# Chunked RWKV-7 scan on TensorE: operands laid out by each head's partition half, and products issued over four 64x64 tiles of the array

## The chip, the cores and the metric

The kernel runs on one core of a Trainium2 chip. A core has a matrix engine (TensorE, PE in the rows), whose weight loads are shown apart as PEld, two engines for elementwise work that can read the matrix engine's result memory PSUM (VectorE or DVE, and ScalarE or ACT), one that works only on SBUF here (GpSimd, POOL), and DMA queues. The metric is the time of one execution in microseconds (us) on the device; lower is better.

## The reference

Two layers of a hybrid backbone over 256 latent and 256 context tokens, width 1024: an input projection feeds three mixers (a bidirectional RWKV-7 scan, attention, a Fourier mix), then a gated merge, an output projection and a feed-forward part. Only the scan is touched by the change. It has 8 heads of width 64, runs in both directions, first over the context, then over the latent tokens from the state reached:

```
def step(S, inp):
    r_t, w_t, k_t, v_t, kk_t, b_t = inp
    sa = -jnp.einsum("bhvk,bhk->bhv", S, kk_t)
    S = S * w_t[:, :, None, :] + sa[..., None] * b_t[:, :, None, :] + v_t[..., None] * k_t[:, :, None, :]
    return S, jnp.einsum("bhvk,bhk->bhv", S, r_t)
S, ys = lax.scan(step, state0, xs, reverse=reverse)
```

The latent stream is returned. The context's outputs y are needed in layer 0 only; in layer 1 the context steps carry the state alone.

## The kernel before, in words

The function scan (from L998) is run once for each of the two layers. It takes the tokens in chunks of 64, so there are 8 steps in a scan (4 context, 4 latent), 16 in all, and each step handles one chunk of each of the two directions d = 0 and 1. A head takes 64 of the 128 partitions, and two heads are a pair: the even head of a pair is on partitions 0 to 63 (UP), the odd one on 64 to 127 (DOWN), and 4 pairs lie side by side. PSUM has 8 banks; direction d owns banks 4d+0 to 4d+3, called B_L, B_LT, B_G, B_S.

One step, for both directions in turn, is on TensorE:

1. **Gram products** (helper `each`, L1259): per pair and head, 64x64 tiles that stay in their partition half (rows UP to outputs UP, DOWN to DOWN). B_LT takes a 128-column product per head, B_L a 64-column one, B_G a 128-column one. Each f32 product is two matmul instructions in the trace, so 8 heads x 2 = 16 instructions for each of the three.
2. **Transposes** (L1296) that turn the decayed keys (BK) token-major into B_S, full 128x128; those of the values (L1305) come later.
3. **The inverse of a unit triangular 64x64 matrix per head**, by merging blocks: T2 holds the inverse and its transpose. The first level is made by DVE (L1198, L1200). Then for levels 1 to 4: X1 = LM x T2 (16 instructions per direction, L1259), ScalarE copies X1 to SBUF (L1120), then two merge products T2 x X1 and X1 x T2 (32 instructions per direction, L1259), and DVE subtracts both from T2 (L1212). The level's mask LM is made by GpSimd (L1064). Level 5 works on 32x32 halves (L1272) and ends in L1217.
4. **The tail**: W = [Q | Gram] x [State ; V] with both parts stacked over all 128 partitions (L1333), ScalarE copies it (L1137); the same stack gives y (L1339); sa = T x W (L1259), copied negated by ScalarE (L1141, two instructions per direction, one for each partition half); y += sa x ARB (L1351); the state product (L1360), stacked over 128 rows and always to outputs UP.
5. DVE adds y (L1236), multiplies the state product by the decay (L1240) and adds the decayed old state (L1243), which GpSimd made at the head of the step (L1056, L1057). These and the stacks need the heads side by side on 64 partitions: tiles QRG, STATE_V, SA_V, BK_TOK, ARB, SD, of which many are written by two instructions, one for each half (`by_head`): L1177 (keep), L1187 (gram_out), L1204, L1141.

All engines follow a program written out by hand in this order; each engine is in order, and semaphores carry the dependences. Within the level loop DVE also does, for direction d, gram_out and keep after levels 1 and 2, the next step's operands(0) (L1168 to L1170) and exponents (L1156, L1157) after the subtraction of level 3, and operands(1) after level 5. ScalarE does its exps (L1088 to L1094) and copies (L1105, L1129, L1134) between the levels. `hold` is a semaphore increment that an engine makes after its waits.

Of the kernel before, what the change touches and what calls it, by code (L numbers as in the profile page):

```python
# [23 lines left out]
ALU = mybir.AluOpType  # L24
AX = mybir.AxisListType

P = 128
# [152 lines left out]
def build_in(ctx, nc, ins, out):  # L180
# [30 lines left out]
    DEC = [sb(f"decay_{d}", [HD, HEADS]) for d in range(NDIR)]  # L211
    DEC_KEPT = [sb(f"decay_kept_{d}", [HD, HEADS]) for d in range(NDIR)]
# [694 lines left out]
    def scratch(*shape):  # L907
# [3 lines left out]
        for i, (mem, at, end) in enumerate(free):  # L911
            if at + n <= end:
# [9 lines left out]
    VF = [scratch(PAIRS, 2, HD) for _ in range(NDIR)]  # L922
    T2 = [scratch(2, PAIRS, HD) for _ in range(NDIR)]
    QRG = [scratch(HEADS, 2, HD) for _ in range(NDIR)]
    STATE_V = [scratch(HEADS, HD) for _ in range(NDIR)]
    SA_V = [scratch(HEADS, HD) for _ in range(NDIR)]
    BK_TOK = [scratch(HEADS, HD) for _ in range(NDIR)]
    ARB = [scratch(HEADS, HD) for _ in range(NDIR)]
    SD = [scratch(HEADS, HD) for _ in range(NDIR)]
# [30 lines left out]
    s_sa_v = [sig(f"values_doubled_{d}") for d in range(NDIR)]  # L960
# [3 lines left out]
    s_add = [sig(f"state_product_decayed_{d}") for d in range(NDIR)]  # L964
    s_ds = [sig(f"state_product_{d}") for d in range(NDIR)]
    s_y_out = [sig(f"y_added_{d}") for d in range(NDIR)]
    s_sd = [sig(f"state_decayed_{d}") for d in range(NDIR)]
# [6 lines left out]
    scan_signals = [s_expo, s_exp, s_init, *s_qr, *s_ops, *s_qr2, *s_gram, *s_lts, *s_gram_out, *s_bk_tok, *s_bk_turned, *s_v_turned, *s_add, *s_v, *s_v_tok, *s_sa_v, *s_lm, *s_x1, *s_x1_out,  # L974
                    *s_tx, *s_t, *s_w, *s_w_out, *s_sa, *s_sa_out, *s_y, *s_ds, *s_y_out, *s_sd, *s_st, *s_first, *s_arb]
# [22 lines left out]
    def scan(context_y):  # L998
# [30 lines left out]
        def of_head(h, half):  # L1029
# [3 lines left out]
        B_L, B_LT, B_G, B_S = 0, 1, 2, 3  # L1033
        by_head = lambda tile, h: (tile.rearrange("p (j h) t -> p j h t", h=2)[:, :, h] if len(tile.shape) == 3 else
                                   tile.rearrange("p (j h) q t -> p j h q t", h=2)[:, :, h])
        pairs = lambda bank, a: BANK[:, bank, a:a + HALF].rearrange("p (j t) -> p j t", j=PAIRS)
        with stage() as block:
            @block.gpsimd
            def _(pool):
                def operands(i, t, d):  # L1040


                    pool.wait_ge(*at_step(s_gram[d], i, 3))
# [5 lines left out]
                def step(i, need_y, more):  # L1049
                    t = [tokens(pool, d, i + 1) for d in range(NDIR)] if more else None  # L1050
                    for d in range(NDIR):

                        pool.wait_ge(*at_step(s_st[d], i))
                        pool.wait_ge(*at_step(s_exp, i, 2, d + 1))
                        hold(pool, "pool")
                        nc.gpsimd.tensor_copy(DEC_KEPT[d][:], DEC[d][:])  # L1056
                        s_sd[d].mark(nc.gpsimd.tensor_tensor(SD[d][UP], STATE_V[d][UP], DEC[d][:].unsqueeze(2).to_broadcast([HD, HEADS, HD]), ALU.mult))  # L1057
# [1241 lines left out]
```

## Time and profile before

| quantity | value |
|---|---|
| median of 3 runs | 2362.63 us (2360.34 to 2364.29) |
| the profiled execution | 2364.6 us, of which the span is 2362.8 us |
| granted TensorE clock over the span, mean | 0.943 |
| busy: PE / PEld / DVE / ACT / POOL | 88% / 70% / 49% / 35% / 14% |
| windows that hold the 16 scan steps, both layers | 513.1 us |

A row of a timeline gives the start, the duration of the merged group, engine, line, operation, tiles written and read, the shape and the count; the bracket is the idle time of the engine just before it and what ended it. A group of pipelined instructions lasts from the first one's start to the last one's end.

### The profile page before, as it was taken

What the parts mean: (1) busy time and instruction counts of PE and PEld (TensorE: products, weight loads), DVE (VectorE), ACT (ScalarE), POOL (GpSimd) and SP (SyncE); (2) the same over time, 40 slices, a digit from 0 to 9 for tenths busy, and PEclk for the clock granted to TensorE, in tenths of its full rate; (3) what the DMA queues carried; (4) which work ended last, traced back from release to release, by engine and by line L of the source; (5) the groups of instructions that cost most, each with busy time, mean ns of one, the idle gap of its engine ahead of it and who ended that gap; (6) DMA issues with size and microseconds to landing.
All of it is one profiled execution on the core that took longest, in us unless ns stands there. A gap on an engine that the chain in (4) does not pass through costs nothing. (4 is left out here: it accounts for less than half of the span.)

```text
span 2362.8 us, 46800 instructions
## 1 busy us (share of the span) xinstructions
PE 2087.1 (88%) x19559; PEld 1657.3 (70%) x19559; DVE 1169.0 (49%) x1849; ACT 832.9 (35%) x1515; POOL 340.5 (14%) x444
## 2 busy tenths in 40 slices
PE   4886888879989999889998998968888798988998
PEld 2653888843557887668886665748887456988988
DVE  1644778762562333253332216377877435545544
ACT  1343444423442222242221114354443244434432
POOL 1112333301100011010001001043332020010000
PEclk8997999989989999999999998979999899999999
DMA  7425000030111332223226743000001211553553
GB/s 263 152 85 200 1 0 2 1 127 13 36 51 49 92 106 89 72 71 107 90 89 238 282 154 125 27 2 0 1 1 44 96 36 56 170 179 125 185 172 126
DMA packets 144521, 219.40 MB, mean 93 GB/s; under 512 B 6846, under 2 KB 123800, under 8 KB 137216
## 3 DMA queue, kind: packets, MB, share of 16 engines
q1 hardware_dynamic: 142880, 215.74, 26.9%
q8 instruction: 101, 1.65, 0.3%
q0 software_dynamic: 1504, 1.71, 0.2%
q14 instruction: 36, 0.29, 0.0%
HBM read 208.00 MB, written 9.44 MB: 92 GB/s over the span
## 5 line engine op out<-in xcount | busy, mean ns | idle before, releaser
L367 PE MATMUL BANK<-H_high,W_high 128*128 128x512 f32 (+2 forms) x1472 | 524.2, 356 | 70.6 <-ACT H_high L630 32.3
L331 DVE TENSOR_TENSOR W_low<-RING,W_high 128x1024 fp32r<-128x1024 f32 x268 | 328.2, 1234 | 461.9 <-ACT W_high L328 461.9
L368 PE MATMUL BANK<-H_low,W_high 128*128 128x512 f32 (+2 forms) x1472 | 520.0, 353 | 0.0
L369 PE MATMUL BANK<-H_high,W_low 128*128 128x512 f32 (+2 forms) x1472 | 519.0, 353 | 0.0
L328 ACT ACTIVATE W_high<-RING 128x1024 fp32r<-128x1024 f32 x268 | 279.3, 1052 | 613.8 <-PE BANK L369 585.9
L367 PEld LDWEIGHTS BANK<-H_high,W_high 128*128 128x128 f32 (+1 forms) x1472 | 283.8, 193 | 117.0 <-issue 50.5
L368 PEld LDWEIGHTS BANK<-H_low,W_high 128*128 128x128 f32 (+1 forms) x1472 | 284.0, 193 | 38.0 <-issue 1.1
L369 PEld LDWEIGHTS BANK<-H_high,W_low 128*128 128x128 f32 (+1 forms) x1472 | 283.7, 193 | 38.0
L1259 PE MATMUL BANK<-RING,WORK 64*64 64x64 f32 x4096 | 166.4, 220 | 16.7 <-DVE RING L1212 8.8
L1259 PEld LDWEIGHTS BANK<-RING,WORK 64*64 64x64 f32 x4096 | 145.2, 134 | 29.2 <-issue 29.0
L1064 POOL TENSOR_TENSOR WORK<-WORK,masks 128x256 f32<-128x256 f32 x160 | 125.5, 796 | 116.5 <-PE BANK L1259 114.7
L367 PE MATMUL BANK<-hidden_high,W_high 128*128 128x512 f32 (+1 forms) x352 | 122.4, 348 | 12.0 <-PEq L2066 12.0
L368 PE MATMUL BANK<-hidden_low,W_high 128*128 128x512 f32 (+1 forms) x352 | 120.0, 341 | 0.0
L369 PE MATMUL BANK<-hidden_high,W_low 128*128 128x512 f32 (+1 forms) x352 | 120.0, 341 | 0.0
L1259 PE MATMUL BANK<-WORK,RING 64*64 64x64 f32 x2560 | 108.1, 225 | 3.1 <-issue 0.7
L2004 POOL TENSOR_TENSOR merge_tiles<-merge_tiles 128x512 f32<-128x512 f32 (+1 forms) x32 | 33.9, 1068 | 480.7 <-DVE merge_tiles L1986 480.7
L1120 ACT ACTIVATE WORK<-BANK 128x256 f32<-128x256 f32 (+1 forms) x160 | 56.5, 362 | 131.5 <-PE BANK L1259 123.5
L1259 PEld LDWEIGHTS BANK<-WORK,RING 64*64 64x64 f32 x2560 | 93.9, 139 | 8.3 <-issue 6.8
L1212 DVE TENSOR_TENSOR RING<-RING,BANK 128x512 f32<-128x512 f32 x128 | 83.7, 683 | 31.9 <-PE BANK L1259 29.1
L1259 PE MATMUL BANK<-RING 64*64 64x128 f32 (+1 forms) x1536 | 79.5, 263 | 21.1 <-DVE RING L1170 21.1
L367 PEld LDWEIGHTS BANK<-hidden_high,W_high 128*128 128x128 f32 x352 | 67.9, 193 | 34.9 <-issue 27.7
L1259 PEld LDWEIGHTS BANK<-RING 64*64 64x64 f32 x1536 | 75.6, 141 | 22.9 <-issue 21.9
(281 smaller groups left out, 3113.9 us busy)
## 6 DMA issues: line engine op xcount, KB each, us to landing
modulation_weights<-w_mod_dram SPq DMA_DIRECT2D x48, 1024.0 KB, 6.7
RING<-w_in_dram SPq DMA_DIRECT2D x46, 1024.0 KB, 5.9
RING<-w_ffn_in_dram SPq DMA_DIRECT2D x44, 1024.0 KB, 5.1
RING<-w_ffn_out_dram SPq DMA_DIRECT2D x20, 1024.0 KB, 5.1
RING<-w_out_dram SPq DMA_DIRECT2D x8, 1024.0 KB, 5.3
h_high<-H_high SPq DMA_DIRECT2D x2, 2048.0 KB, 7.5
h_low<-H_low SPq DMA_DIRECT2D x2, 2048.0 KB, 13.2
H_high<-h_high SPq DMA_DIRECT2D x2, 2048.0 KB, 11.8
```

What stands on the lines that cost most here:

```text
L328: high_ready.mark(nc.scalar.activation(self.part(0, c), self.raw(c), ACT.Copy))
L331: low_ready.mark(nc.vector.tensor_tensor(self.part(1, c), self.raw(c), self.part(0, c).bitcast(FP32), ALU.subtract))
L367: nc.tensor.matmul(out, w[0], x[0], start=start, stop=False)
L368: nc.tensor.matmul(out, w[0], x[1], start=False, stop=False)
L369: return nc.tensor.matmul(out, w[1], x[0], start=False, stop=stop)
L1064: s_lm[d].mark(nc.gpsimd.tensor_tensor(LM[d], LTS[d], lanes(level_mask(d, l)), ALU.mult))
L1120: s_x1_out[d].mark(nc.scalar.activation(X1[d][:, :, cols], pairs(4 * d + B_L, 0)[:, :, cols], ACT.Copy))
L1212: s_t[d].mark(nc.vector.tensor_tensor(T2[d].rearrange("p q j t -> p (q j t)"), T2[d].rearrange("p q j t -> p (q j t)"), BANK[:, 4 * d + B_ ...
L1259: last = nc.tensor.matmul(BANK[rows, bank, at + j * stride:at + j * stride + width], lhs(j)[rows], rhs(j)[rows], start=True, stop=True)
L2004: pool_sig.mark(nc.gpsimd.tensor_tensor(total(m), total(m), gate(u), ALU.add))
```

## The change

The stacks over 128 partitions are given up. Each tile of the scan keeps the even heads of the pairs on one partition half and the odd ones on the other, so most copies and elementwise instructions that were two of 64 partitions become one of 128 partitions with half the elements per partition. What was one product over K = 128 becomes two accumulated products over K = 64, one of each head's own half and one whose operands have the heads of a pair exchanged (GRAM_X, V_X, the second half of BK_TOK, and the transposed inverse T2[:, 1]). The helper side_by_side interleaves up to two products, pair by pair. A product is given by the pair (rows, outputs): STAY reads and writes the same half, CROSS goes from the own half to the other, BACK from the other to the own, STAY_OTHER is STAY with the halves named the other way round. A STAY and a CROSS (or BACK) product together use all four 64x64 tiles of the array, in two banks.

The transposes become products with an identity (eye_heads). The state decay is one multiplication by DVE after one addition, and GpSimd's two instructions per direction (L1056, L1057) are gone. New waits of TensorE on its own products: s_turned_1, s_turned_2, s_w_1, s_y_1, s_y_2, s_ds_1, and two on the first gram product.

```diff
-                for h, rows in enumerate((UP, DOWN)):
-                    last = nc.vector.tensor_copy(by_head(QRG[d][UP], h), QR[d][rows])
-                s_qr2[d].mark(last)
+                s_qr2[d].mark(nc.vector.tensor_copy(QR_KEPT[d], QR[d]))
...
-                s_sd[d].mark(nc.gpsimd.tensor_tensor(SD[d][UP], STATE_V[d][UP], DEC[d][:].unsqueeze(2).to_broadcast([HD, HEADS, HD]), ALU.mult))
...
+                        if l >= 4:
+                            d = l - 4
+                            act.wait_ge(*at_step(s_st[d], i))
+                            s_dec[d].mark(nc.scalar.activation(DEC[d][:].unsqueeze(2), INCL[d][:, :, bass.ds(here[d] + (CHUNK - 1), 1)], ACT.Exp, scale=-KAPPA))
...
-                        s_add[d].mark(nc.vector.tensor_tensor(STATE_V[d][UP], BANK[UP, 4 * d + B_S].rearrange("p (g t) -> p g t", g=HEADS),
-                                                              DEC_KEPT[d][:].unsqueeze(2).to_broadcast([HD, HEADS, HD]), ALU.mult))
+                        s_add[d].mark(nc.vector.tensor_tensor(STATE[d], STATE[d], pairs(4 * d + B_S, 0), ALU.add))
...
-                        s_st[d].mark(nc.vector.tensor_tensor(STATE_V[d][UP], STATE_V[d][UP], SD[d][UP], ALU.add))
+                        s_st[d].mark(nc.vector.tensor_tensor(STATE[d], STATE[d], DEC[d][:].unsqueeze(2).to_broadcast([P, PAIRS, HD]), ALU.mult))
...
+                OWN, OTHER = (UP, DOWN), (DOWN, UP)
+                STAY, CROSS, BACK, STAY_OTHER = (OWN, OWN), (OWN, OTHER), (OTHER, OWN), (OTHER, OTHER)
+                def side_by_side(width, *products):
+                    last = [None] * len(products)
+                    for j in range(PAIRS):
+                        for x, (bank, at, (rows, to), lhs, rhs, start, stop) in enumerate(products):
+                            for h in range(2):
+                                last[x] = nc.tensor.matmul(BANK[to[h], bank, at + j * width:at + (j + 1) * width], lhs(j)[rows[h]], rhs(j)[rows[h]],
+                                                           start=start and (j == 0 or stop), stop=stop and (j == PAIRS - 1 or start))
+                    return last
...
+                    first_free(0)
+                    s_gram[0].mark(side_by_side(HD, lower(0))[0])
+                    wide(0)
+                    first_free(1)
+                    pe.wait_ge(*at_step(s_gram[0], i, 4, 1))
+                    across, straight = side_by_side(HD, upper_across(0), lower(1))
+                    wide(1)
+                    pe.wait_ge(*at_step(s_gram[1], i, 4, 1))
+                    across, straight = side_by_side(HD, upper_across(1), (B_S, 0, STAY, bk(0, 0), eye, True, True))
+                    pe.wait_ge(*at_step(s_turned_1, i, 1, 1))
+                    across, straight = side_by_side(HD, (B_S, HALF, CROSS, bk(0, 1), eye, True, True), (4 + B_S, 0, STAY, bk(1, 0), eye, True, True))
+                    pe.wait_ge(*at_step(s_turned_2, i, 1, 1))
+                    s_bk_turned[1].mark(side_by_side(HD, (4 + B_S, HALF, CROSS, bk(1, 1), eye, True, True))[0])
...
+                        if l >= 4:
+                            s_ds_1[d].mark(side_by_side(HD, (4 * d + B_S, 0, BACK, lambda j: BK_TOK[d][:, 1, j], lambda j: V_X[d][:, j], True, False))[0])
...
-                                each(4 * d + B_LT, 0, HD, lambda j: T2[d][:, 1, j], lambda j: X1[d][:, j])
-                                s_tx[d].mark(each(4 * d + B_LT, HALF, HD, lambda j: X1[d][:, j], lambda j: T2[d][:, 1, j]))
+                                s_tx[d].mark(side_by_side(HD, (4 * d + B_L, 0, STAY_OTHER, lambda j: X1[d][:, j], lambda j: T2[d][:, 1, j], True, True),
+                                                          (4 * d + B_LT, 0, BACK, lambda j: T2[d][:, 1, j], lambda j: X1[d][:, j], True, True))[1])
...
+                    s_w_1.mark(side_by_side(HD, w_own(0, True), w_other(1, True))[1])
+                    if need_y:
+                        s_y_1.mark(side_by_side(HD, y_own(0, True), y_other(1, True))[1])
+                    pe.wait_ge(*at_step(s_w_1, i, 1, 1))
+                    one, zero = side_by_side(HD, w_own(1, False), w_other(0, False))
+                    if need_y:
+                        s_y_2.mark(side_by_side(HD, y_own(1, False), y_other(0, False))[1])
...
-                            last = nc.tensor.matmul(BANK[UP, 4 * d + B_S, g * HD:(g + 1) * HD], BK_TOK[d][:, g], SA_V[d][:, g],
-                                                    start=True, stop=True)
+                        s_ds[d].mark(side_by_side(HD, (4 * d + B_S, 0, STAY, lambda j: BK_TOK[d][:, 0, j], lambda j: SA[d][:, j], False, True))[0])
```

wide(d) is the side-by-side form of the two 128-column gram products (B_LT by STAY, B_G by CROSS), 32 instructions. B_LT and B_L have changed numbers (0 and 1), and T2's first level is now read from B_L alone, where the transposed part lies in the second half of the bank with the heads exchanged.

## Rows read from the trace of the kernel before

**Rows 1.** The page: busy time by engine, over the whole span.
```profile
PE 2087.1 (88%) x19559; PEld 1657.3 (70%) x19559; DVE 1169.0 (49%) x1849; ACT 832.9 (35%) x1515; POOL 340.5 (14%) x444
```

**Rows 2.** Windows, one scan step each: us, busy by engine, granted clock, DMA.
```profile
323.50:356.00 32.50, 29.12 (x723) 26.87 (x721) 24.39 (x43) 13.73 (x36) 11.71 (x16) 0.95 0.00 0
418.90:450.10 31.20, 27.68 (x724) 25.47 (x720) 24.45 (x43) 13.73 (x36) 11.71 (x16) 1.00 0.00 0
1664.00:1693.50 29.50, 25.89 (x667) 23.81 (x664) 24.02 (x42) 13.73 (x36) 11.72 (x16) 1.00 0.00 0
```

**Rows 3.** Timeline of one step, its head: gram products, first level, transposes.
```profile
418.37 4.40 PEld L1259 LDWEIGHTS BANK<-RING 64*64 64x64 f32 x96
...
422.95 0.85 PEld L1296 LDWEIGHTS BANK<-ident,RING 128*128 128x128 f32 x8 [0.17 <-issue]
423.64 0.60 ACT L1105 ACTIVATE WORK<-BANK 128x512 f32<-128x512 f32 x1 [1.01 <-PE BANK L1296]
424.35 0.42 PEld L1305 LDWEIGHTS BANK<-ident,RING 128*128 128x128 f32 x4 [0.55 <-issue]
424.94 0.54 PEld L1259 LDWEIGHTS BANK<-RING,WORK 64*64 64x64 f32 x16 [0.17 <-issue]
```

**Rows 4.** Timeline, levels 1 to 3 of the same step.
```profile
425.67 0.38 ACT L1120 ACTIVATE WORK<-BANK 128x256 f32<-128x256 f32 x1 [1.43 <-PE BANK L1259]
426.47 0.58 PEld L1259 LDWEIGHTS BANK<-WORK,RING 64*64 64x64 f32 x16
426.94 0.58 PEld L1259 LDWEIGHTS BANK<-RING,WORK 64*64 64x64 f32 x16
427.79 0.69 DVE L1212 TENSOR_TENSOR RING<-RING,BANK 128x512 f32<-128x512 f32 x1 [1.13 <-PE BANK L1259]
428.68 0.57 PEld L1259 LDWEIGHTS BANK<-RING,WORK 64*64 64x64 f32 x16 [0.23 <-issue]
429.34 1.39 DVE L1187 TENSOR_TENSOR RING<-BANK,masks 64x512 f32<-64x512 f32 x2
430.77 0.90 DVE L1177 COPY RING<-RING 64x512 f32<-64x512 f32 x2
431.70 1.28 DVE L1212 TENSOR_TENSOR RING<-RING,BANK 128x512 f32<-128x512 f32 x2
432.60 1.08 PEld L1259 LDWEIGHTS BANK<-RING,WORK 64*64 64x64 f32 x32 [0.20 <-issue]
```

**Rows 5.** Timeline, level 4 of the same step and the start of level 5.
```profile
436.45 1.08 PEld L1259 LDWEIGHTS BANK<-RING,WORK 64*64 64x64 f32 x32 [0.63 <-issue]
436.75 0.42 DVE L1168 TENSOR_TENSOR RING<-WORK 128x256 f32<-128x256 f32 x1
439.16 0.41 DVE L1157 TENSOR_TENSOR WORK<-WORK 128x256 f32 x1
440.38 0.86 PEld L1272 LDWEIGHTS BANK<-RING,WORK 32*32 32x32 f32 x32 [0.71 <-issue]
441.98 0.53 PEld L1272 LDWEIGHTS BANK<-RING,WORK 32*32 32x32 f32 x32 [0.74 <-issue]
```

**Rows 6.** Timeline, the tail of the same step.
```profile
442.55 1.01 PEld L1333 LDWEIGHTS BANK<-WORK,RING 128*64 128x64 f32 x32
444.56 1.01 PEld L1259 LDWEIGHTS BANK<-WORK,RING 64*64 64x64 f32 x32
445.29 1.56 ACT L1141 ACTIVATE WORK<-BANK 64x256 f32<-64x256 f32 x4 [1.16 <-PE BANK L1259]
447.61 1.94 PEld L1360 LDWEIGHTS BANK<-WORK 128*64 128x64 f32 x32
```

**Rows 7.** Windows of 1 us around level 5 of an earlier step.
```profile
344.00:345.00 1.00, 0.44 (x15) 0.30 (x11) 1.00 (x3) 0.77 (x3) 0.00 (x0) 1.00 0.00 0
346.00:347.00 1.00, 0.36 (x27) 0.39 (x29) 0.00 (x0) 0.95 (x4) 0.63 (x1) 1.00 0.00 0
349.00:350.00 1.00, 1.00 (x24) 1.00 (x20) 0.53 (x2) 0.00 (x0) 0.00 (x0) 0.50 0.00 0
```

More of the change, by code:

```diff
@@ L210, in build_in @@
     g2_sb = sb("g2_sb", [P, WIDTH])
-    DEC = [sb(f"decay_{d}", [HD, HEADS]) for d in range(NDIR)]
-    DEC_KEPT = [sb(f"decay_kept_{d}", [HD, HEADS]) for d in range(NDIR)]
+    DEC = [sb(f"decay_{d}", [P, PAIRS]) for d in range(NDIR)]
     BANK = ctx.enter_context(nc.psum_tensor("BANK", [P, 8, 512], FP32))
@@ L921, in build_in @@
     BK = [scratch(PAIRS, 2, HD) for _ in range(NDIR)]
-    VF = [scratch(PAIRS, 2, HD) for _ in range(NDIR)]
+    VF = [scratch(PAIRS, HD) for _ in range(NDIR)]
     T2 = [scratch(2, PAIRS, HD) for _ in range(NDIR)]
[L924 to L929, printed above, removed]
+    QR_KEPT = [scratch(PAIRS, 2, HD) for _ in range(NDIR)]
+    GRAM_X = [scratch(PAIRS, 2, HD) for _ in range(NDIR)]
+    STATE = [scratch(PAIRS, HD) for _ in range(NDIR)]
+    V_X = [scratch(PAIRS, HD) for _ in range(NDIR)]
+    SA = [scratch(PAIRS, HD) for _ in range(NDIR)]
+    BK_TOK = [scratch(2, PAIRS, HD) for _ in range(NDIR)]
+    ARB = [scratch(PAIRS, HD) for _ in range(NDIR)]
     EXPO = scratch(2, PAIRS, HD)
@@ L1139, in step @@
                         act.wait_ge(*at_step(s_sa[d], i, 1, 1))
-                        for h, rows in enumerate((UP, DOWN)):
-                            last = nc.scalar.activation(by_head(SA_V[d][UP], h), pairs(4 * d + B_LT, 0)[rows], ACT.Copy, scale=-1.0)
-                        s_sa_out[d].mark(last)
+                        s_sa_out[d].mark(nc.scalar.activation(SA[d], pairs(4 * d + B_LT, 0), ACT.Copy, scale=-1.0))
                 for d in range(NDIR):
@@ L1271, in halves @@
                             k = of_head(h, k_rows)
-                            last = nc.tensor.matmul(BANK[of_head(h, out_rows), bank, at + j * HD + out_cols.start:at + j * HD + out_cols.stop],
+                            last = nc.tensor.matmul(BANK[of_head(h ^ across, out_rows), bank, at + j * HD + out_cols.start:at + j * HD + out_cols.stop],
                                                     lhs[k, j, out_rows], rhs[k, j, out_cols], start=True, stop=True)
@@ L1303, in step @@
                             hold(pe)
-                            for j in range(PAIRS):
-                                last = nc.tensor.transpose(BANK[:, 4 * d + B_S, j * P:(j + 1) * P], VF[d][:, j].rearrange("p q t -> p (q t)"), ident[:])
-                            s_v_turned[d].mark(last)
+                            turned = side_by_side(HD, (4 * d + B_S, 0, CROSS, lambda j: VF[d][:, j], eye, True, True))
+                            s_v_turned[d].mark(turned[0])
+                        if l >= 4:
+                            d = l - 4
+                            pe.wait_ge(*at_step(s_v_tok[d], i, 1, 1))
+                            hold(pe)
+                            s_ds_1[d].mark(side_by_side(HD, (4 * d + B_S, 0, BACK, lambda j: BK_TOK[d][:, 1, j], lambda j: V_X[d][:, j], True, False))[0])
                         for d in range(NDIR):
```

153 lines of the change are left out of this document (69 added, 84 removed).

## The prediction

> **What bounds the kernel now.** I read the page first, then windows, then the timeline of one step. TensorE is busy 2087 of 2363 us [rows 1], but in the scan this hides short waits: the windows give 31.2 us for a step at full clock, 32.5 us for one in which the clock was down to 0.95 in the mean, and 29.5 us for a context step of layer 1, which makes no y [rows 2]. DMA moves nothing there. The 16 steps take 513.1 us, 22% of the run, and nothing outside them changes.
>
> The timeline shows a chain, no single busy engine. From the first gram load to the first load of X1 it is 424.94 - 418.37 = 6.57 us [rows 3]. Levels 1 to 4 take 3.74, 3.92, 3.85 and 3.93 us (starts at 424.94, 428.68, 432.60, 436.45, 440.38) [rows 3 to 5], level 5 takes 442.55 - 440.38 = 2.17, and the tail to the next gram product, which follows the state product's end at 447.61 + 1.94, takes 7.05 [rows 5, 6]. Together 31.2 us, the window's length.
>
> **Durations used.** From these rows: a group of 16 matmuls of 64 columns goes out in 426.94 - 426.47 = 0.47 us, 29 ns each [rows 4]. From its first load to ScalarE's copy 425.67 - 424.94 = 0.73 passes, so 0.26 beyond the issue; a copy lasts 0.38 [rows 3, 4]. I add 0.11 from a copy to TensorE (an estimate: about half of DVE's step, below). The two merge groups take 0.94, and DVE starts 1.32 after their first load, so 0.38 beyond the issue; one subtraction is 0.69, two are 1.28, and from its end (428.48) to TensorE's load 0.20 passes [rows 4].
>
> **The unknown: how fast four tiles take matmuls.** Before, groups use two tiles at a time. Three rows bound it. On one column half over all 128 rows (L1360) 32 matmuls take 1.94 us, 61 ns; alternating column halves (L1333) 32 take 1.01, 32 ns with the last one's latency in it; 32-wide ones alternating between two tiles take 0.53 for 32, 16.6 ns [rows 5, 6]. So a second tile halves the interval, two column halves stream different operands over the same rows, and loads and matmuls can leave at 16.6 ns or faster. What no row shows is two row halves that write the same PSUM partitions in different banks at once. Ends: 16.6 ns (issue is then the limit; streaming alone would be 61/4 = 15) and 29 ns (only two tiles ever work). I take 16.6, since L1333 and the L1259 groups each show one of the two directions of the tiling running side by side. A group of 32 then takes 0.53 instead of 0.94, and the 128-column pair, where 96 matmuls took 4.40 [rows 3], so (2.20 - 0.47)/32 = 54 ns each, takes 27 ns x 32 = 0.87 instead of 1.73.
>
> The Trainium skill (TensorE: Matmul & The Clock Gate, section "Wait — 56ns, not 53.3ns?") says that start-to-start never drops below about 25 ns however small the matmul. The L1272 row has 16.6 ns, so the trace does not agree; by the page's floor a merge group would take 0.80, and that is a rival below.
>
> **The change part by part,** a warm latent step:
>
> *Head.* TensorE issues lower(0) 0.47, wide(0) 0.87, upper(0) with lower(1) 0.53, wide(1) 0.87, upper(1) with the first turn 0.53, then a wait on its own product, the second turn 0.53. The self-waits have no row; bounds are 0 and the 0.64 of result latency plus wake-up seen through another engine (0.38 + 0.26); I take 0.35. Sum 4.15. Then ScalarE's copy of BK (0.26 + 0.60 + 0.11 [rows 3]) and the value product 0.47: X1 starts at 5.6 instead of 6.57. T2 is not late: DVE's state update is 4 instructions of 128x256 (0.42 each, as L1168 [rows 5]) instead of 4 of 64x512, and done before wide(1) ends; the first level for d = 0 waits for upper(0) at 1.87 + 0.38, plus two 128x512 instructions of 0.69 = 3.6. GpSimd's mask for level 1 no longer stands behind the state decay. Gain 1.0.
>
> *Levels 1 to 3.* Chain of d = 0: 0.73 + 0.38 + 0.11 + 0.53 + 0.38 + 0.69 + 0.20 = 3.0 us instead of 3.84 in the mean. Of this 0.4 comes from four tiles; the rest was DVE, which reached L1212 late behind gram_out (1.39) and keep (0.90) [rows 4]. These become one instruction each (0.69 + about 0.5), and 1.28 + 1.19 = 2.5 is under the 3.0 of the chain. The second value product sits in TensorE's idle time. Sum 9.0 instead of 11.5; gain 2.5.
>
> *Level 4.* DVE makes operands and exponents before the subtraction: 436.75 to 439.57, 2.82 us [rows 5], unchanged. 1.28 + 2.82 = 4.1: DVE now bounds this level, instead of 3.93. Gain -0.2. The first part of the state product (2 x 0.47) is hidden in TensorE's waiting here; if uncovered it costs 0.9.
>
> *Level 5.* The second product starts 441.98 - 440.38 = 1.60 after the first; the chain alone (0.26 + 0.26 + 0.38 + 0.11) is 1.0. The rest is ScalarE copying SA_V (L1134), which the change removes. Its replacement, one 128x4 exponential per direction, is short. 2.17 - 0.6 = 1.6; gain 0.6.
>
> *Tail.* W takes two groups of 32 with a y group between: W is ready at 3 x 0.53 + 0.26 = 1.85, later than before (0.47 + 0.26). Copy and wake-up 2.35, sa 0.47 + 0.26, its copy is one instruction (0.38) instead of two per direction (1.56 for four [rows 6]), y from 3.57 on 0.94, the state product 2 x 0.47 instead of 1.94. End 5.45 instead of 7.05; gain 1.6. The self-waits on y_1 and w_1 find their product done, except w_1 in a context step without y (0.35).
>
> Sum: 5.6 + 9.0 + 4.1 + 1.6 + 5.45 = 25.8 instead of 31.2, so 5.4 us a step. A step without y saves 4.7 (the y groups it never had, one exposed wait). 12 x 5.4 + 4 x 4.7 = 84 us.
>
> **The clock.** A step whose granted clock fell cost 1.3 us more [rows 2]. It fell to 0.50, which is 1.2 of 2.4 GHz, for some 3 to 4 us after a stretch in which TensorE was busy 0.44 and 0.36 of a microsecond [rows 7]. 8 of the 16 windows show it. The change thins out TensorE's time in the levels (0.94 + 1.06 us of issue in 3.0, instead of 2.8 in 3.85). I count it in all 16 steps: 8 x 1.35 = 11 us back. The profiled execution's 2364.6 less 84 plus 11 is 2292; the median of the runs is 2 us below that execution, and the rate of four tiles is more likely a little under 16.6 ns than over. Forecast 2288 us, 3.2% faster.
>
> **Rivals.**
>
> 1. *Four tiles give nothing* (the change does not do what it says): 29 ns. Head: 0.47 + 1.73 + 0.94 + 1.73 + 0.94 + 0.35 + 0.94, then 1.44 to X1, is 8.5. Levels 1 to 3: 3.44 each, 10.3; level 4 4.1; level 5 1.6; tail 4 x 0.94 + 0.73 + 0.38 + 0.11 + 1.88 = 6.9. Sum 31.4: all that DVE and ScalarE gain is eaten by 208 more matmuls (by the diff, 928 instructions a step instead of 720: the turns 96 instead of 16, W, y and the state product twice as many, the gram 128 instead of 96). 0.2 us a step more with y, about nothing without: 2362 to 2375, with the clock's loss. Against: the rows of L1333. Chance 0.08, half of it within 0.2%, half above.
>
> 2. *An issue floor of 25 ns.* Head 0.47 + 0.87 + 0.80 + 0.87 + 0.80 + 0.35 + 0.80 + 1.44 = 6.4; levels 3.3 each; tail 6.2; sum 28.2, 3.0 us a step, about 2330 with the clock. The Trainium skill's floor (same page) is this case. Against: L1272. For: its burst is short, and nothing shows such a rate held. Chance 0.07.
>
> 3. *Slower: the clock.* If TensorE's thinner work left it at 1.2 GHz for most of each step, everything TensorE issues on the chain doubles: about 4.2 + 0.5 in the head, 1.0 in each of four levels, 3.9 in the tail, 12 to 13 us. The step would be 38, the run 2364.6 + 16 x 6.5 = 2470. It decides from the point where 5.4 of these 12.5 us are lost, so when the low clock holds for over 40% of the scan. Against: in the warm window level 5 has the same thin stretches and 1.00 [rows 2, 5], and each fall seen was over in 4 us [rows 7]. Chance 0.04.
>
> 4. *Better than the sum:* 13 to 15 ns per matmul, no fall of the clock added, and exponents not slowed by GpSimd's work beside them (2.82 us for five 0.42 instructions): another 1 to 1.5 us a step, 2265. That is inside the forecast's own case.
>
> **How the numbers follow.** Forecast with its spread 0.78, floor 0.07, clock 0.04, no gain 0.08, and 0.03 for a stall of TensorE or DVE that I do not see, half of it slower. The range reaches from 2255 (rival 4 with 10 us more) to 2335 (rival 2), and leaves out rivals 1 and 3 and the tails of the forecast. Faster by over 0.2% (4.7 us, about what a measurement of this kernel can tell from none): 0.78 + 0.07 + 0.015 = 0.86; within 0.05; slower 0.09.
>
> **What would show it.** In the changed trace a merge group (32 matmuls of 64x64, BANK<-WORK,RING and RING,WORK mixed) lasts about 0.55 us of loads; 1.0 would be rival 1, 0.8 rival 2. Starts of X1 in consecutive levels 3.0 us apart, 4.1 in level 4 with DVE busy throughout; the tail 5.5. Idle PE of about 0.35 after the first and second turned groups. Wrong would be made by a copy of BK on ScalarE that waits longer than the turns, by a first level on DVE later than 5.4, or by windows with a clock under 0.9.

## The result, and the profile of the changed kernel

The changed kernel takes 2486.43 us (median of 4 runs, 2485.28 to 2488.03) beside 2361.78 us for the kernel before, measured with it: a ratio of 1.053 (95%: 1.051 to 1.055), 5.3% slower. The forecast was 2288 us, its range 2255 to 2335, and "faster" had a chance of 0.86. It was wrong in sign, and by 198 us.

The page of the changed kernel: busy time by engine [rows 1], the line of the granted clock in 40 slices, and the queue that brings instructions.

```profile
PE 2090.4 (84%) x22759; PEld 1659.7 (67%) x22759; DVE 1066.6 (43%) x1753; ACT 774.6 (31%) x1419; POOL 296.8 (12%) x380
...
PEclk8997778988998999999999999867878899998999
...
q8 instruction: 201, 3.29, 0.6%
```

The page of the kernel before, the same two last lines (the first stands in rows 1):

```profile
PEclk8997999989989999999999998979999899999999
...
q8 instruction: 101, 1.65, 0.3%
```

DVE, ScalarE and GpSimd lost the busy time that the change meant to take from them (DVE 1169.0 to 1066.6). TensorE has the same busy sum, 2090 beside 2087, with 3200 more matmuls, which fits four tiles at work. Still the span grew by 121 us, and the instruction queue moved twice as much: 201 packets, 3.29 MB, 16 KB each.

Windows of the two scans and of three single steps (columns as in rows 2: us, busy of PE, PEld, DVE, ACT, POOL, granted clock, DMA share, GB/s). The first two lines are the scans; then, from gram load to gram load, a context and a latent step of layer 0, both with y, and a context step of layer 1, without.

```profile
224.40:538.40 314.00, 226.13 (x7424) 208.67 (x7425) 141.37 (x286) 79.78 (x237) 72.93 (x97) 0.84 0.02 4
1625.20:1939.30 314.10, 226.20 (x7047) 208.60 (x7048) 141.21 (x283) 79.53 (x236) 73.77 (x97) 0.79 0.02 4
...
328.73:373.97 45.24, 29.99 (x928) 27.83 (x928) 16.72 (x36) 10.08 (x30) 8.59 (x13) 0.77 0.02 4
373.97:409.56 35.59, 26.84 (x921) 24.85 (x919) 16.82 (x36) 10.08 (x30) 8.75 (x12) 0.86 0.01 3
1641.52:1680.69 39.17, 26.83 (x839) 24.66 (x836) 17.93 (x34) 10.09 (x30) 9.40 (x13) 0.74 0.02 4
```

The scans take 628.1 us instead of 515.1 (259.1 and 256.0 by the same windows of before), so nearly all of the 121 us is there. The steps shown are 36 to 45 us, where 25.8 had been worked out and 31.2 measured [rows 2]. No engine is busy for more than 30 us of a step.

The waits of TensorE, over the whole span (engine, line, what was waited for: us in all, times, longest):

```profile
PE BANK L1248 <- issue: 129.4, 81, 4.7
...
PE BANK L1257 <- issue: 8.9, 8, 1.5
```

"Issue" is idle time for which no semaphore answers: 138 us, in pieces of up to 4.7 us; all such waits on the scan's lines come to 1.3 us in the kernel before. One piece in detail, in windows of 1 us, two finer windows over the idle time itself, and the timeline (start, us, engine and line, what, and in brackets the wait before it):

```profile
377.00:378.00 1.00, 1.00 (x55) 0.88 (x46) 0.76 (x2) 0.00 (x0) 0.32 (x1) 1.00 0.06 16
...
381.00:382.00 1.00, 1.00 (x32) 1.00 (x33) 0.00 (x0) 0.50 (x2) 0.80 (x2) 0.50 0.00 0
383.00:384.00 1.00, 1.00 (x36) 1.00 (x31) 0.92 (x2) 0.28 (x2) 0.50 (x1) 0.50 0.09 16
...
377.80:378.20 0.40, 0.22 (x8) 0.08 (x4) 0.40 (x2) 0.00 (x0) 0.00 (x0) 1.00 0.14 41
378.20:380.20 2.00, 0.00 (x0) 0.00 (x0) 2.00 (x6) 0.00 (x0) 0.00 (x0) 1.00 0.00 0
```

```profile
377.24 1.28 DVE L1188 TENSOR_TENSOR RING<-RING,BANK 128x512 f32<-128x512 f32 x2 [1.51 <-PE BANK L1248]
380.21 1.53 PEld L1248 LDWEIGHTS BANK<-RING,WORK 64*64 64x64 f32 x34 [2.33 <-issue]
381.03 0.38 ACT L1105 ACTIVATE WORK<-BANK 128x256 f32<-128x256 f32 x1 [4.04 <-PE BANK L1248]
384.27 0.27 PEld L1257 LDWEIGHTS BANK<-RING,WORK 32*32 32x32 f32 x12
386.19 0.45 PEld L1257 LDWEIGHTS BANK<-RING,WORK 32*32 32x32 f32 x20 [1.66 <-issue]
```

TensorE stops for 2.33 us between the first state product and the X1 products of level 4. The only thing that it waits for there is DVE's subtraction, and both of these are done by 378.52; ScalarE, whose 4.04 us also hold its usual wait, stands idle with it. The next stop, 1.66 us, lies in the middle of a group of level 5: 12 loads, the gap, then 20 more with the same operands and no wait between them. A packet of 16 KB starts as the first stop begins (the windows count its bytes where it starts; its own record ends at 378.76), and TensorE goes on 1.4 us after its end. That is no chance: each of the 31 gaps of over 0.9 us between weight loads in this scan (228 to 538 us) ends 1.2 to 1.6 us after the end of a packet of the instruction queue, while these packets come some 5 us apart. After the stop the granted clock falls from 1.00 to 0.50, so the same matmuls take twice as long: 55 matmuls began in the microsecond before the gap, 32 and 36 behind it. That named the suspect, the transport of TensorE's own instructions, and the experiments test it.

### The profile page after: what moved, and what is told of

Read it like the earlier page. It is cut to its first block and busy times, and to the rows that moved or that the text cites. A ratio compares the mean times of both kernels' runs of the same rounds, so it can differ in the third digit from the quotient of the medians.

```text
span 2483.5 us, 52924 instructions
## 1 busy us (share of the span) xinstructions
PE 2090.4 (84%) x22759; PEld 1659.7 (67%) x22759; DVE 1066.6 (43%) x1753; ACT 774.6 (31%) x1419; POOL 296.8 (12%) x380
## 3 DMA queue, kind: packets, MB, share of 16 engines
q8 instruction: 201, 3.29, 0.6%
## 5 line engine op out<-in xcount | busy, mean ns | idle before, releaser
L1248 PE MATMUL BANK<-RING,WORK 64*64 64x64 f32 x4480 | 193.1, 239 | 35.4 <-issue 22.9
L1248 PE MATMUL BANK<-RING 64*64 64x64 f32 (+1 forms) x2944 | 134.6, 308 | 88.4 <-issue 65.1
L1248 PEld LDWEIGHTS BANK<-RING,WORK 64*64 64x64 f32 x4480 | 172.4, 150 | 48.2 <-issue 46.7
L1248 PEld LDWEIGHTS BANK<-RING 64*64 64x64 f32 x2944 | 124.8, 189 | 92.9 <-issue 92.6
L1248 PE MATMUL BANK<-WORK,RING 64*64 64x64 f32 x3072 | 157.8, 257 | 26.7 <-issue 23.1
L1056 POOL TENSOR_TENSOR WORK<-WORK,masks 128x256 f32<-128x256 f32 x160 | 119.4, 759 | 426.3 <-ACT WORK L1097 273.7
L1248 PEld LDWEIGHTS BANK<-WORK,RING 64*64 64x64 f32 x3072 | 134.1, 166 | 35.1 <-issue 34.9
## 6 DMA issues: line engine op xcount, KB each, us to landing
h_low<-H_low SPq DMA_DIRECT2D x2, 2048.0 KB, 12.5
```

Source lines behind the costliest of these rows:

```text
L1056: s_lm[d].mark(nc.gpsimd.tensor_tensor(LM[d], LTS[d], lanes(level_mask(d, l)), ALU.mult))
L1248: last[x] = nc.tensor.matmul(BANK[to[h], bank, at + j * width:at + (j + 1) * width], lhs(j)[rows[h]], rhs(j)[rows[h]], start=start and (j ...
```

## The experiments

**Theory.** The step loop's body, 720 matmuls of code before, is 928 now. It no longer stays on the core, so it is fetched again in every step, and TensorE runs dry. **Rivals:** the clock (rival 3 of the forecast: TensorE's thinner work, not its code); the four tiles themselves (the exchanged halves or two row halves at once); other work of the change.

**The same instructions executed, less code.** Levels 2 to 4 have the same text for TensorE, so they can be an inner loop. 928 matmuls are executed and 736 stand in the code. The order changes a little too: the second value turn moves ahead of the loop, the first part of the state product behind it.

```
+ values_turned(0); level(1, True, False); values_turned(1)
+ Signal.trips = trips * (NL - 2)
+ with pe.Fori(2, NL) as l:
+     level(l, False, False)
+ Signal.trips = trips
+ state_product_first(0); state_product_first(1); level(NL, False, True)
```

> The changed kernel, with TensorE's merge levels 2 to 4 written as an inner loop (three trips of one body of 96 matmul instructions) instead of three copies; the second value turn moved ahead of that loop, the first part of the state product behind it. TensorE executes the same 928 matmul instructions a step, but its step body holds 736 of them in code, near the 720 of the kernel before. Theory 1 (the step's code is too long to stay on the core, is fetched again in every iteration, and TensorE waits for its instructions): instruction packets of queue q8 back to about 100 (201 in the changed kernel), TensorE's idle time with the releaser 'issue' under 2 us a step (5 to 15 now), step 26 to 27 us, time 2290 us, between 2270 and 2320. Theory 2 (the new order itself is slow: waits on own products, four tiles, a thinner load on the clock): no change to 2486, within 20 us.

Measured: 2320.83 us (2312.02 to 2326.64) beside 2367.31, ratio 0.981 (0.977 to 0.985): 166 us less than the changed kernel (171, if each is taken from the kernel before of its own batch, 2361.78 and 2367.31). That is 1 us above the range expected. The page's instruction queue, TensorE's waits, the first scan and one later step:

```profile
q8 instruction: 101, 1.65, 0.3%
...
PE BANK L1248 <- issue: 19.7, 29, 2.3
...
223.10:453.80 230.70, 195.52 (x7424) 182.58 (x7424) 148.44 (x286) 80.29 (x237) 75.55 (x97) 0.94 0.01 1
379.08:406.30 27.22, 24.25 (x928) 22.76 (x928) 18.69 (x38) 10.22 (x30) 9.21 (x12) 0.94 0.00 0
```

The first scan executes the same 7424 matmuls in 230.70 us instead of 314.00, the idle time by issue goes from 138 to 20 us, the packets are back at 101 and the clock at 0.94 instead of 0.84. That refutes the tiles as the cause, and the clock as an independent one: the work is as thin as in the changed kernel, and the low clock went with the gaps. That it is the length and not the changed order is shown further down, by a variant that has this order and a longer body.

**No step loop at all,** in the changed kernel and in the kernel before: every step's code stands once, in a row.

```
-                with eng.Fori(first, end) as i:
-                    step(i, need_y, True)
+                for i in range(first, end):
+                    step(i, need_y, True)
```

> The changed kernel with no loop over the steps: all 16 steps are straight code, so every instruction is fetched once, none is fetched after a jump back. Theory 1a (what costs is the jump back to code that is gone): stalls go, time 2300 to 2340. Theory 1b (what costs is the rate of fetching, 928 x 2 instructions of 64 bytes in 25 us): the stalls stay, one for each 16 KB or so, step 33 to 36 us as in the changed kernel's straight last step, time 2430 to 2490. Theory 2: 2486, without a word on fetches.

> The kernel before with no loop over the steps: the same work, but every step's code is fetched. Theory 1: instruction packets about 165 instead of 101; the code goes out at 720 x 2 instructions in 31 us, slower than in the changed kernel; a small loss of 0 to 1 us a step, 2362 to 2380. If fetching alone makes the 13 us stalls whatever the rate: 2450 or more. Theory 2: 2362, no change at all.

Measured: the changed kernel 2414.83 us (2409.78 to 2416.88), ratio 1.020 (1.017 to 1.023); the kernel before 2363.56, ratio 0.999 (0.997 to 1.001). The first lies between what was expected of the jump back alone (2300 to 2340) and of the rate of fetching (2430 to 2490), so either may have a part; the second is as expected. Their instruction queues, the changed kernel first, and its main wait:

```profile
q8 instruction: 182, 2.98, 0.5%
...
PE BANK L1248 <- issue: 96.9, 88, 2.6
```

```profile
q8 instruction: 157, 2.57, 0.5%
```

Three readings. The two kernels differ by 3200 matmuls and 0.41 MB, so a matmul with its load is 128 B of code: the body is 92 KB before, 119 KB changed. Code that is fetched in a row costs the kernel before nothing in time (its waits by issue are 6.9 us), but the changed one 106 us of idle time (96.9 and 8.9): fetching keeps up with 720 matmuls in 31 us and not with 928 in 26. And the loop is worse than no loop, 2486 beside 2415 us, with more packets (201 beside 182) although no more is executed. In the straight code, too, all 33 gaps of over 0.9 us in the first scan end 1.2 to 1.6 us after the end of a packet.

The Trainium skill (Runtime: NRT & Kernel Launch, section "Instruction fetch mechanics") says that the sequencer fetches code in blocks of 16 KiB, 256 instructions, one after another while it executes, which is "mostly hidden", and that a taken branch to a target outside the current window of two such blocks forces a fetch before execution goes on. The packets of 16 KB and the 128 B for a load and a matmul agree; "mostly hidden" holds for the kernel before (6.9 us in straight code) and not for the changed one (106 us). The window of two blocks does not fit: the body of 92 KB loops with no packet (rows 2, DMA 0.00). The fetch behind the branch fits the loop's being slower than the row where the body did not stay, with pieces of up to 4.7 us instead of 2.6.

**The code's length alone, in the kernel before.** 208 small matmuls (32x32, results unused and no part of the computation) go into each step ahead of level 5: written out, 928 in the code; then the same from a loop of 8 trips, 746 in the code.

```
+ if l == NL:
+     for x in range(104):     # in the second: with pe.Fori(0, 8): for x in range(13)
+         at = 64 * (x % 2)
+         nc.tensor.matmul(BANK[at:at + 32, B_L, HALF:HALF + 32], ident[at:at + 32, at:at + 32], ident[at:at + 32, at:at + 32], start=True, stop=True)
```

> The kernel before with 208 small matmul instructions more a step (104 products of 32x32 with the identity into an unused part of PSUM, results unused), written out ahead of level 5, so that a step's code holds 928 of them as in the changed kernel while its own work and order are untouched. Theory 1: the code no longer stays on the core; instruction packets about 200, idle by 'issue' 5 us or more a step, together 60 to 120 us slower than the same kernel with the additions in a loop (e6). Theory 2 (only the changed kernel's order suffers): equal to e6.

> The control of e5: the same 208 small matmul instructions are executed at the same place, but from a loop of 8 trips over 26 of them, so the step's code holds 746. Theory 1: instruction packets about 105, no stalls; 1.5 to 2.8 us of additional matmuls a step, less what they fill of TensorE's wait, plus the loop's jumps: 2385 to 2420. Theory 2: as e5.

Measured: 2524.76 us, ratio 1.068 (1.066 to 1.071), and 2433.48 us, ratio 1.029 (1.026 to 1.031). The queue and the longest wait by issue of the first, and the queue of the second:

```profile
q8 instruction: 205, 3.36, 0.6%
...
PE BANK L1259 <- issue: 46.2, 23, 4.1
```

```profile
q8 instruction: 102, 1.67, 0.3%
```

The same matmuls are executed, and 91 us lie between them: the price of length alone, in a kernel that has nothing of the change. All waits by issue on the scan's lines are 71.7 us in the first and 1.9 in the second, so 70 of the 91 are seen as such. The second came 13 us above the upper end of what was expected of it: the 208 matmuls cost 70 us in all, 21 ns each in the mean. That is a miss of the price of the filling, not of the theory, which asked for the difference.

**Where the limit lies.** The same filling with 64 and with 88 matmuls a step (range(32) and range(44)).

> As e5 (the kernel before with small matmuls written out ahead of level 5), with 64 of them: 784 matmul instructions in a step's code. It bounds the limit, which lies between 752 (e4, 102 packets) and 832 (the changed kernel's steps without y, fetched again). Below the limit: 102 to 104 packets, 2365 to 2385; above: 170 or more packets and 2400 or more.

> As e11 with 88 small matmuls: 808 in a step's code. Below the limit: 103 to 106 packets, 2370 to 2395; above: 175 or more packets and 2410 or more.

Measured: 2384.11 us, ratio 1.008 (1.006 to 1.011), and 2403.33 us, ratio 1.017 (1.014 to 1.019). The instruction queues, 784 first:

```profile
q8 instruction: 122, 2.00, 0.4%
```

```profile
q8 instruction: 132, 2.16, 0.4%
```

Neither came out as expected (102 to 106 packets if the body stays, 170 and more if not). Windows of single steps show why the counts lie between. With 808, a context and a latent step of layer 0, both from a body of 808:

```profile
305.80:347.30 41.50, 33.73 (x808) 31.38 (x808) 23.24 (x43) 13.73 (x36) 11.27 (x17) 0.88 0.02 4
423.20:454.50 31.30, 28.82 (x812) 26.73 (x810) 24.49 (x43) 13.73 (x36) 11.70 (x16) 1.00 0.00 0
```

With 784, a context and a latent step of layer 0:

```profile
292.00:331.10 39.10, 31.52 (x784) 29.11 (x784) 23.27 (x43) 13.71 (x36) 11.29 (x16) 0.91 0.02 4
433.30:464.50 31.20, 28.38 (x789) 26.29 (x785) 24.45 (x43) 13.72 (x36) 11.72 (x16) 1.00 0.00 0
```

It is one loop of several, and in it all of the body. With 808 the repeated steps of layer 0's context loop take 43.1, 41.5 and 41.9 us and bring 9, 9 and 8 packets; with 784 they take 31.3, 39.1 and 38.1 and bring 2, 9 and 8. The latent loops of both layers have the same number of matmuls in their code; their repeated steps bring none and take 31.2 to 32.8 us, as in the kernel before (31.2 at full clock, rows 2), so there the filling itself costs nothing. The 20 and 39 us are for the most part two and three steps that are 6 to 10 us longer than in the kernel before (13 and 29 us), and not a small price on every step. At 752 (the run below, 102 packets) the body stays in every loop, at 928 in none (8 to 10 packets a repeated step); at 784 and 808 both occur. Length alone does not decide in between, and what does is not shown; where the body begins within the blocks of 16 KB was not varied.

The same section of the Trainium skill gives TensorE 128 KiB. Each of these bodies is shorter, down to the 100 KB of 784, so a loop cannot count on the whole of it.

**An inner loop that is too short.** Levels 2 and 3 alone as the inner loop: 832 matmuls in the code of a step with y, 736 without.

```
-                    with pe.Fori(2, NL) as l:
+                    with pe.Fori(2, 4) as l:
                         level(l, False, False)
+                    level(4, False, False)
```

> The inner-loop kernel of e1 with the inner loop over levels 2 and 3 only and level 4 written out: 832 matmul instructions in the code of a step with y, 736 in one without. The straight kernel's steps without y (832 in code) were fetched again each time. Theory 1: the steps without y in layer 1 run as in e1 (27.4 us each, no fetch), those with y are fetched again and take 32 to 42 us: 101 + about 50 to 60 packets, 2320 + 10 x 5 to 12 us = 2370 to 2440. If the limit were above 832 after all: 2321 as e1.

Measured: 2429.87 us (2421.65 to 2439.59), ratio 1.029 (1.026 to 1.032). Its queue, then GpSimd's first instruction of two consecutive context steps without y (layer 1) and of two steps with y (layer 0):

```profile
q8 instruction: 160, 2.62, 0.5%
...
1648.14 0.73 POOL L1046 TENSOR_TENSOR RING<-WORK 128x256 f32<-128x256 f32 x1 [0.41 <-ACT WORK L1082]
1675.45 0.73 POOL L1046 TENSOR_TENSOR RING<-WORK 128x256 f32<-128x256 f32 x1 [0.39 <-ACT WORK L1082]
```

```profile
279.51 0.72 POOL L1046 TENSOR_TENSOR RING<-WORK 128x256 f32<-128x256 f32 x1 [0.55 <-ACT WORK L1082]
320.27 0.72 POOL L1046 TENSOR_TENSOR RING<-WORK 128x256 f32<-128x256 f32 x1 [0.54 <-ACT WORK L1082]
```

One kernel holds both cases: 27.3 us for a step whose body is 736, 40.8 us for one whose body is 832. It is not the y: in the first variant, where both bodies are within 736, steps without and with y take 27.3 and 27.2 us. Nor is it the order of the instructions, which is that of the first variant: 96 matmuls more in the code are the only difference, and they cost 109 us.

**One part alone.** The kernel before with the merge products on four tiles and the exchanged inverse, and for that one more gram product per direction: 752 matmuls in the code. Everything else is as it was.

```
- each(4 * d + B_LT, 0, HD, lambda j: T2[d][:, 1, j], lambda j: X1[d][:, j])
- s_tx[d].mark(each(4 * d + B_LT, HALF, HD, lambda j: X1[d][:, j], lambda j: T2[d][:, 1, j]))
+ s_tx[d].mark(side_by_side(HD, (4 * d + B_L, 0, STAY_OTHER, lambda j: X1[d][:, j], lambda j: T2[d][:, 1, j], True, True),
+                           (4 * d + B_LT, 0, BACK, lambda j: T2[d][:, 1, j], lambda j: X1[d][:, j], True, True))[1])
```

> The kernel before with one part of the change: the transposed inverse kept with the heads of a pair exchanged, and the merge products of levels 1 to 4 side by side on four tiles (one more gram product per direction, 752 matmul instructions in the step's code instead of 720). Everything else (layout, stacks, DVE and ScalarE work) as before. Theory 1: if 752 still stays on the core, instruction packets about 105 and no stalls; a merge group takes 0.55 us instead of 0.94, of which DVE's late subtractions leave about 0.2 us a level; the added gram product with its own wait costs 0.5 to 1.0; 2350 to 2370. If 752 is over the limit: packets about 180 and 2420 or more. Theory 2 (four tiles slow TensorE or its clock): slower than 2375 with packets at 105.

Measured: 2376.91 us (2374.65 to 2387.02), ratio 1.006 (1.004 to 1.009). A miss: 2350 to 2370 had been expected. Over 2375 with packets at 105 had even been named as the sign that four tiles slow TensorE or its clock; 102 packets and 2 us over that mark are too little to tell, and the next experiment speaks against it. The main wait of TensorE:

```profile
PE BANK L1276 <- DVE RING L1212: 35.9, 46, 1.4
```

The faster products now wait for DVE, whose work by partition halves is still the old one, 54.5 us in all with those of level 5 (18.1 in the kernel before), and the repeated steps with y last some 31 to 33 us as before. Four tiles give nothing as long as DVE sets the levels: this part needs the other one. Why it came out slightly slower rather than equal was not pursued; its waits by issue, 12.8 us beside 1.3, are of the size of the 9.6 us that it lost.

**The four tiles alone.** The first variant (inner loop) with the products of a group one after the other instead of interleaved:

```
-                        for j in range(PAIRS):
-                            for x, (bank, at, (rows, to), lhs, rhs, start, stop) in enumerate(products):
+                        for x, (bank, at, (rows, to), lhs, rhs, start, stop) in enumerate(products):
+                            for j in range(PAIRS):
```

> The inner-loop kernel of e1, with side_by_side issuing its two products one after the other (all pairs of the first, then all of the second) instead of interleaved, so that two tiles work at a time. The same instructions, 736 in code. If four tiles carry a part of the gain: a merge group takes 0.94 us instead of 0.46; the level period 3.05 becomes 3.5, the head grows by about 3, the tail by 1 to 2; step 31 to 33 us, time 2380 to 2420. If the array does nothing more with four tiles: 2321 as e1.

Measured: 2346.58 us (2344.61 to 2353.42), ratio 0.993 (0.991 to 0.996), where 2380 to 2420 had been expected. A steady step, then the 64 loads of a level's merge products in this variant and in the first:

```profile
389.55:419.00 29.45, 27.22 (x930) 25.73 (x928) 18.71 (x37) 10.19 (x30) 9.18 (x12) 1.00 0.00 0
...
391.30:392.68 1.38, 1.33 (x62) 1.36 (x64) 0.80 (x2) 0.65 (x2) 1.16 (x2) 1.00 0.00 0
...
401.65:402.63 0.98, 0.91 (x61) 0.94 (x64) 0.05 (x1) 0.97 (x3) 0.98 (x2) 1.00 0.00 0
```

The interleaving is worth 29.45 - 27.22 = 2.2 us a step and 26 us in all; at the same clock of 1.00 (the variant below, 26.47) it is 3.0. 31 to 33 us a step had been expected (rival 1's sum is 31.4). One reason is in the windows: 64 loads take 1.38 us, not the 1.9 of two tiles (29 ns each) and not the 0.98 of the interleaved form, so in this variant successive products still overlap in part, and it does not hold TensorE to two tiles. 2.2 us is thus a lower bound for what four tiles are worth, and 31.2 to 29.45 is what the change gains without the interleaving.

**The clock by itself.** The inner-loop kernel with three products of 128x256 (6 matmuls, results unused) where TensorE would wait, two before level 5 and one between its products:

```
+ def filler(n):
+     for _ in range(n):
+         nc.tensor.matmul(BANK[:, B_S, HALF:2 * HALF], ident[:], masks[:, 0, 0:4].rearrange("p q t -> p (q t)"), start=False, stop=False)
```

> The inner-loop kernel of e1 with three more products of 128x256 a step (6 matmul instructions of about 0.2 us, results unused): two behind the first part of the state product, where TensorE waits for DVE in level 4, one between the two products of level 5. They test whether the thin work there is what takes the clock down in the tail (in e1 the loads of W go from 14 to 27 ns each 0.4 us into the group). If so: the tail shrinks by 1.0 to 1.3 us, less up to 0.4 us by which the fillers delay level 5; time 2300 to 2315. If the clock falls anyway: 2321 plus up to 8.

Measured: 2317.68 us (2315.17 to 2320.71), ratio 0.980 (0.978 to 0.982); a steady step:

```profile
382.43:408.90 26.47, 23.90 (x934) 21.79 (x934) 18.69 (x38) 10.10 (x30) 9.20 (x12) 1.00 0.00 0
```

The step's clock is 1.00 instead of 0.94 and it takes 26.47 us instead of 27.22. Over the whole run the gain is 3 us and lies within the spread of both kernels; 2300 to 2315 had been expected.

**The shortest code.** Levels 1 to 4 in the inner loop, the second value turn behind level 4, two fillers: some 644 matmuls in the code.

```
- Signal.trips = trips * (NL - 2)
- with pe.Fori(2, NL) as l:
-     level(l, False, False)
+ Signal.trips = trips * (NL - 1)
+ with pe.Fori(1, NL) as l:
+     level(l, True, False)
```

> The kernel of e8 with its inner loop over all four levels 1 to 4 (640 matmul instructions in a step's code instead of 736, plus two filler products: one behind the first state product of direction 0, one between the two products of level 5); the values of direction 1 are turned behind level 4, and ScalarE's copy of them follows there. Theory 1 goes on: what is left of 'issue' idle time (20.6 us in e8) comes from the first pass of each loop and the straight last steps, and falls with the code's length: packets 101 to about 90, idle 12 to 18 us, time 2305 to 2316. If the added order costs more in level 4 than it saves: 2318 to 2330.

Measured: 2315.64 us (2312.05 to 2323.79), ratio 0.981 (0.978 to 0.983), 97 packets where some 90 were expected, 13.6 us of issue. With the two above it is the best version, 1.9% faster than the kernel before; the three can't be told apart.

## Why the prediction was wrong, point by point

**The step that failed** is the count under "Rivals" and the sum that rests on it: "208 more matmuls (by the diff, 928 instructions a step instead of 720)". They were priced as work that TensorE executes, and rightly. They are also 27 KB more code in the body of a loop, and that had no term in the sum. The sentence before it, "DMA moves nothing there", was read off the windows [rows 2] and was true: it was the sign that the old body stayed on the core, and I didn't ask up to which length. The last clause of the chances, 0.03 for "a stall of TensorE or DVE that I do not see", was all that stood for it.

Its size: the two scans take 628.1 us changed and 461.4 with the shorter code, 167 us, the whole difference of the two kernels (166). TensorE's idle time by issue differs by 138 - 20 = 118 of it; the other 49 are not measured by themselves. The clock can hold them: at a mean of 0.84 and 0.79 instead of 0.94 and 0.92, some 165 us more of the scans lie at the low level, where the matmul groups take twice as long.

**What held,** read in the kernel with the inner loop, whose instructions are the changed kernel's. One steady step there, 394.99 to 422.21, beside the sum: head to X1 5.46 us (forecast 5.6); levels 1 to 3 at 3.06, 3.05 and 3.04 (3.0); level 4 at 3.91, bound by DVE (4.1); level 5 1.95 (1.6); tail 6.75 (5.45). In all 27.22, and 25.8 + 1.35 for the clock was 27.15. The total is closer than its parts: apart from the clock they are off by -0.14, +0.15, -0.19 and +0.35 us, which nearly cancel. The chain behind the 3.0 us shows in the timeline, DVE's subtractions of two consecutive levels:

```profile
405.63 1.28 DVE L1188 TENSOR_TENSOR RING<-RING,BANK 128x512 f32<-128x512 f32 x2 [0.32 <-PE BANK L1248]
408.68 1.28 DVE L1188 TENSOR_TENSOR RING<-RING,BANK 128x512 f32<-128x512 f32 x2 [0.32 <-PE BANK L1248]
```

**The rate of four tiles** was taken as 16.6 ns. In the changed kernel, at full clock:

```profile
376.87 0.14 PEld L1248 LDWEIGHTS BANK<-WORK,RING 64*64 64x64 f32 x2
376.89 0.17 PEld L1248 LDWEIGHTS BANK<-RING,WORK 64*64 64x64 f32 x2
376.93 0.14 PEld L1248 LDWEIGHTS BANK<-WORK,RING 64*64 64x64 f32 x2
376.94 0.17 PEld L1248 LDWEIGHTS BANK<-RING,WORK 64*64 64x64 f32 x2
```

Four loads every 0.058 us, 14.6 ns each (64 of them go out from 376.36 to 377.28). That is better than the lower end, refutes rival 1 (29 ns), and rival 2 with the floor of 25 ns that the Trainium skill states (TensorE: Matmul & The Clock Gate, section "Wait — 56ns, not 53.3ns?"). The self-waits were 0.27 and 0.30 us, where 0.35 was taken.

**The tail** came out 1.3 us longer than its sum, and this is the clock: in the step of the inner-loop kernel it falls at 415.86, early in the tail.

```profile
415.57 0.17 PEld L1248 LDWEIGHTS BANK<-RING 64*64 64x64 f32 x2
415.63 0.17 PEld L1248 LDWEIGHTS BANK<-RING 64*64 64x64 f32 x2
...
416.10 0.24 PEld L1248 LDWEIGHTS BANK<-RING 64*64 64x64 f32 x2
416.21 0.24 PEld L1248 LDWEIGHTS BANK<-RING 64*64 64x64 f32 x2
```

The interval doubles from 0.06 to 0.11 us; 0.50 is 1.2 of 2.4 GHz. The forecast had put that loss beside the parts, 1.35 us in every step, so the parts' error and the clock's term are one thing. The variant with the fillers shows it: its tail, at full clock, takes 5.57 us where 5.45 was the sum.

```profile
392.02:397.59 5.57, 5.25 (x224) 5.04 (x224) 2.92 (x10) 1.43 (x4) 0.00 (x0) 1.00 0.00 0
```

**Rival 3** gave 2470 us, near the 2486 measured, and its condition was nearly met: a mean clock of 0.84 and 0.79 is 32% and 42% of the scans at the low level, against 40%. The number is close for another reason. Its cause was thin work; the inner-loop kernel has the same work and 0.94. The low clock came with the gaps and went with them, and 118 of the 166 us are the gaps themselves. Who had only compared the time would have taken that rival for confirmed. (Its sum is also off: it adds 6.5 us a step where its own terms, 12.5 less 5.4, give 7.1, so 2478 us.)

**The remaining 33 us** between the forecast and the inner-loop kernel: 20 us are issue waits, in first passes through the loops and in the straight last steps, where code comes for the first time; the repeated steps with y are as forecast. Of the other 13, some 5 are in the four steps without y, which take 27.3 us at a clock of 0.87 where 29.5 - 4.7 + 1.35 = 26.15 had been forecast, and 5.5 are in the batch: its kernel before took 2367.31 us, not 2361.78. With this kernel's 2321 us the range would have held.

**Open.** Why a loop over a body that is too long costs more than the same code in a row (2486 and 2415 us; with y, steps of 45 us in the first loop of layer 0, 35 in its second) is not settled, nor what decides between two loops of the same length at 784 and 808. The branch back, if nothing is fetched ahead behind it, fits and is not shown. It is not shown either whether the limit counts bytes or instructions; the fillings and the variants had only loads and matmuls to vary.

## What to carry to other kernels

Count a change's instructions twice, as work and as code: beside "how long do they take" stands "does the loop body that holds them still stay on the core". The signs are the instruction queue's packets on the page, equal before and after or not, and TensorE's waits by "issue". A count in between can mean one loop of several, so look at the steps of each. Where a body nears the limit, look for a stretch that repeats in it (here the levels of a merge tree) and let it be an inner loop: that gave back 166 us and made a 5.3% loss a 1.9% gain, with no work changed. Unrolling doesn't help when the engine executes faster than code arrives.

## What the runs showed of the hardware that I had not expected

- A loop body on TensorE stayed on the core at 752 matmuls of code in every loop (102 packets of 16 KB in the run) and in none at 928 (201 and 205). At 784 (122) and 808 (132) it was brought again whole in one loop of layer 0, 8 or 9 packets and 6 to 10 us a step, and stayed in the two latent loops of the same length. A matmul with its load is 128 B.
- At 928 the length cost 91 us in one kernel and 166 in the other, whose step is faster.
- A TensorE that lacks its instructions goes on 1.2 to 1.6 us after the end of a packet of the instruction queue: 31 of 31 gaps of over 0.9 us in the changed kernel's first scan.
- Straight code was free at 720 matmuls in 31 us, some 3 KB per us, and short of supply at 928 where 26 us were wanted, some 4.6 KB per us.
- Matmuls of 64x64 on four tiles leave every 14.6 ns at full clock, and every 27 ns at half.
- Six unused matmuls in TensorE's idle time held the clock at 1.00 through a step and shortened it by 0.75 us.
